# The gates' projection of a one-layer block: f32 products against three products of rounded parts

## The reference, cut to what matters

```
hx = modulate(rms_norm(x), shift, scale)       # 256 tokens x 2048
hc = modulate(rms_norm(ctx), ...)              # 256 context tokens x 2048
px = hx @ w_in                                 # 2048 x 10720
pc = hc @ w_in[:, :MIX_IN]
g_a, g_b = split(px[..., MIX_IN:], 2)          # the gates: 4096 columns, latent tokens only
yx_a = rwkv7_mixer(px[..., :RWKV_IN], ...)     # needs the final state of the context scan
yx_b = gla_mixer(px[..., RWKV_IN:MIX_IN], ...)
m = sigmoid(g_a) * (yx_a @ w_rwkv_up) + sigmoid(g_b) * (yx_b @ w_gla_up)
x = x + gx1 * rms_norm(m @ w_out)
x = x + gx2 * rms_norm(swiglu(modulate(rms_norm(x), ...)))
```

## Time and profile before

| | us |
|---|---|
| median of 3 runs | 2163.39 (2159.5 to 2163.41) |
| the profiled execution, its own time | 2161.05 |
| its span, first to last instruction | 2159.3 |
| PE busy in the span | 2020.6 (94%) |
| GLA phase, PE's first gates product to its last | 579.7 to 770.1 |
| preparation, first product to the last stored | 773.2 to some 924 |

### The profile page before, as it was taken

The page is one execution under the profiler, slowest core; times in us unless marked ns, Lnnn a source line. Parts: engine busy times, 40 slices in busy tenths (PEclk is TensorE's granted clock), DMA queues, the critical chain, the costliest instruction groups (busy, mean ns, idle before and its releaser), DMA issues. The chain is left out here.

```text
span 2159.3 us, 35926 instructions
## 1 busy us (share of the span) xinstructions
PE 2020.6 (94%) x15475; PEld 1651.2 (76%) x15475; DVE 1245.3 (58%) x1150; ACT 808.1 (37%) x895; POOL 249.9 (12%) x125
## 2 busy tenths in 40 slices
PE   5899999999999989967889899999999999999998
PEld 3367888888788866656788688778888888888886
DVE  3355666665556347768888486554445455444445
ACT  2232111212263235445554465443334333433333
POOL 0023121312304034301000020000000000000000
PEclk9899999999999999989999999999999999999999
DMA  8988889887554389967442678536555555555553
GB/s 305 382 284 313 315 316 322 290 318 270 153 143 124 88 233 312 297 151 195 93 92 57 113 228 323 178 98 192 184 187 194 186 185 192 194 202 192 193 195 115
DMA packets 355505, 453.62 MB, mean 210 GB/s; under 512 B 106062, under 2 KB 261054, under 8 KB 338094
## 3 DMA queue, kind: packets, MB, share of 16 engines
q1 hardware_dynamic: 347760, 440.59, 64.4%
q10 hardware_dynamic: 7614, 11.10, 1.4%
HBM read 413.43 MB, written 38.22 MB: 209 GB/s over the span
## 5 line engine op out<-in xcount | busy, mean ns | idle before, releaser
L220 DVE TENSOR_TENSOR f_w_lo<-t_w_raw,f_w_hi 128x2048 fp32r<-128x2048 f32 x132 | 302.4, 2292 | 361.5 <-ACT f_w_hi L214 361.5
L214 ACT ACTIVATE f_w_hi<-t_w_raw 128x2048 fp32r<-128x2048 f32 x132 | 252.9, 1916 | 436.0 <-PE pf L2926 288.0
L2924 PE MATMUL pf<-f_w_hi,h 128*128 128x512 f32 x704 | 276.3, 392 | 1.5 <-DVE h L2745 1.5
L2925 PE MATMUL pf<-f_w_lo,h 128*128 128x512 f32 x704 | 274.8, 390 | 0.0
L2926 PE MATMUL pf<-f_w_hi,h 128*128 128x512 f32 x704 | 274.7, 390 | 0.0
L214 ACT ACTIVATE p_w_hi<-h_w_raw 128x2048 fp32r<-128x2048 f32 x48 | 89.3, 1910 | 333.2 <-DVE stage L761 252.1
L906 DVE SCALAR_TENSOR_TENSOR late_acc<-h_of_x,siluc,late_acc 128x2048 f32<-128x2048 f32 x60 | 160.6, 2677 | 46.9 <-DMA h_of_x<-in_ada_w 45.2
L2975 PE MATMUL d_out<-f_w_hi,hid 128*128 128x512 f32 x704 | 176.3, 390 | 0.3 <-DVE f_w_lo L220 0.3
L264 PE MATMUL p_in<-h,p_w_hi 128*128 128x512 f32 x448 | 174.3, 389 | 0.0
L266 PE MATMUL p_in<-h,p_w_lo 128*128 128x512 f32 x448 | 174.3, 389 | 0.0
L265 PE MATMUL p_in<-h,p_w_hi 128*128 128x512 f32 x448 | 174.3, 389 | 0.0
(11 more groups left out here) (419 smaller groups left out, 3404.9 us busy)
## 6 DMA issues: line engine op xcount, KB each, us to landing
h_of_x<-in_ada_w SPq DMA_DIRECT2D x64, 1024.0 KB, 5.6
h_w_raw<-in_w_in SPq DMA_DIRECT2D x48, 1024.0 KB, 7.6
t_w_raw<-in_ffn_w_gate SPq DMA_DIRECT2D x44, 1024.0 KB, 5.2
t_w_raw<-in_ffn_w_up SPq DMA_DIRECT2D x44, 1024.0 KB, 5.2
t_w_raw<-in_ffn_w_down SPq DMA_DIRECT2D x44, 1024.0 KB, 4.9
h_w_raw<-in_ada_w SPq DMA_DIRECT2D x32, 1024.0 KB, 10.5
gate_w<-in_w_in SPq DMA_DIRECT2D x30, 1024.0 KB, 6.0
t_w_raw<-in_w_out SPq DMA_DIRECT2D x16, 1024.0 KB, 6.0
```

Of the source, the lines that this page charges most:

```text
L214: act.activation(self.hi[:, m % self.S, 0:w], self.raw[:, s, 0:w], ACT.Copy)\
L220: eng.tensor_tensor(self.lo[:, m % self.S, 0:w], self.raw[:, s, 0:w], b32(self.hi[:, m % self.S, 0:w]), ALU.subtract)\
L2924: pe.matmul(o, h2[:, 0, k, rows], fring.hi[:, s, at], start=k == 0, stop=False)
L2925: pe.matmul(o, h2[:, 0, k, rows], fring.lo[:, s, at], start=False, stop=False)
```

## The change

The gates' products become three products of rounded parts, like the rest.

- `h` is kept through the later phases as its two fp32r parts, in a new order [128, ctx or x, part, 16 k, 256 tokens]. The rejoining (L744, L779) goes. In the input projection, the 512 columns of one part of `h` are now two runs of 256 (ctx and x).
- The gates' weights come in 64 granules of 128x1024 (512 KB, rows of 1 KB): a granule holds 4 k-blocks of two tiles. Each granule is made `hi` by ACT (four of them by DVE) and `lo` in place by POOL (50 of them) or DVE (14). There are five slots for raw granules and three for `hi`: `hi` of granule n waits until granule n-3 is used.
- PE's order: in the GLA phase 96 products ahead of the levels, 16 behind each, 64 behind them, which stand between the output products; in the preparation 48 ahead, 16 in each pair, 32 behind; 16 in the scan. A product is now three instructions of 256 columns.
- In the GLA phase ACT's and DVE's work ahead of the levels is put in another order (both directions' Abs and Exp ahead of both Ln), and the norm behind the levels goes head by head.

```diff
-            hx = alloc(ph_hx, "h_of_x", [P, KT, SEQ])
+            h = alloc(ph_hx, "h", [P, 2, 2, KT, SEQ], f32r)
...
 def phase_w_in(nc, A, env):
...
-                pool.tensor_tensor(hx[:, KH:], b32(h_hi)[:, KH:, CTX:], b32(h_lo)[:, KH:, CTX:], ALU.add).then_inc(s_hx, 1)
...
-                                    last = mm3(pe, o, ring.hi[:, s, at], ring.lo[:, s, at], h_hi[:, kk, ts],
-                                               h_lo[:, kk, ts], kk == 0, kk == KT - 1)
+                                    last = mm3(pe, o.rearrange("p (a t) -> p a t", a=2), ring.hi[:, s, at],
+                                               ring.lo[:, s, at], h[:, :, 0, kk, :], h[:, :, 1, kk, :], kk == 0,
+                                               kk == KT - 1)
...
 class Gates:
...
-    STAGES = 4
-    SCAN = 1
-    AHEAD = 2
+    STAGES, RAW, SPLIT = 4, 5, 3
+    HI_VECTOR = [4, 5, 6, 7]
+    LO_VECTOR = [0] + list(range(13, 28, 2)) + [37, 39, 41, 61, 63]
...
+    def wait_raw(self, eng, n):
...
+        if n >= self.SPLIT:
+            eng.wait_ge(self.used, n - self.SPLIT + 1)
+    def hi(self, act, n):
+        self.wait_raw(act, n)
+        act.activation(self.high[:, n % self.SPLIT], self.place(n), ACT.Copy).then_inc(self.hi_scalar, 1)
+    def lo(self, eng, n):
+        eng.wait_ge(*self.hi_done(n))
+        eng.tensor_tensor(self.low_place(n), self.place(n), b32(self.high[:, n % self.SPLIT]), ALU.subtract)\
+           .then_inc(self.lo_done(n)[0], 1)
...
-            mm = pe.matmul(self.banks[t % nb][:, 0:SEQ], tiles[:, slot, k * P:(k + 1) * P], self.hx[:, k, :],
-                           start=k == 0, stop=k == KT - 1)
+            last = self.mm3(pe, self.banks[(f - self.first) % nb][:, 0:SEQ], self.high[:, n % self.SPLIT, cols],
+                            self.low_place(n)[:, cols], self.h[:, 0, k, :], self.h[:, 1, k, :], k == 0,
+                            k == KT - 1)
...
 def phase_rwkv_pre(nc, A, out, env):
...
             @block.gpsimd
...
+                gates.lo(pool, 38)
                 pool.wait_ge(s_lx, 80)
...
+                gates.lo(pool, 40)
                 neighbours(0)
                 neighbours(1)
+                gates.lo(pool, 42)
+                gates.lo(pool, 43)
                 for j in range(PAIRS):
...
+                    gates.lo(pool, 44 + 2 * j)
...
+                    gates.lo(pool, 45 + 2 * j)
                     if j + 2 < PAIRS:
                         neighbours(j + 2)
...
             @block.scalar
...
                    act.activation(nrm[:, b, :], nrm[:, b, :], ACT.Sqrt).then_inc(s_nrm, 1)
+                    gates.hi(act, 45 + 2 * j)
                     if j + 2 < PAIRS:
                         middle(j + 2)
...
+                    gates.hi(act, 46 + 2 * j)
...
             @block.tensor
             def _(pe):
-                gates.multiply(pe, 0, lead)
+                gates.multiply(pe, 8 * PRE_PARTS, 48)
...
-                    gates.multiply(pe, lead + per * j, per // 2)
+                    gates.multiply(pe, 8 * PRE_PARTS + 48 + 16 * j, 8)
...
 def phase_gla(nc, A, out, env):
...
             @block.gpsimd
...
                 for n in range(LEVELS):
+                    gates.lo(pool, 12 + 2 * n)
                     pool.wait_ge(s_e, 2 * n + 1)
                     pool.tensor_tensor(E[:, n % 2, 0], k[:], E[:, n % 2, 0], ALU.mult).then_inc(s_K, 1)
+                for n in range(28, PRE_PARTS + 1):
+                    gates.lo(pool, n)
...
             @block.scalar
...
                 for n in range(LEVELS):
+                    gates.hi(act, 12 + 2 * n)
                     for part in range(2):
...
+                    gates.hi(act, 13 + 2 * n)
...
             @block.vector
...
                     if n >= 1:
                         select(n - 1, gm[:, n - 1, :].bitcast(mybir.dt.uint32).unsqueeze(1).broadcast_to([P, GH, P]))
+                    gates.lo(dve, 13 + 2 * n)
...
             @block.tensor
...
                     level(n, E[:, n % 2, 0], E[:, n % 2, 1], n == LEVELS - 1)
-                    gates.multiply(pe, 112 + 14 * n, 14)
+                    gates.multiply(pe, 96 + 16 * n, 16)
```

More of the change, by code:

```diff
@@ L634 @@
 GLA_GATES = 18
+GATE_UNITS = [(2 * n, 2) for n in range(KT - 1)] + [(2 * KT - 2, 1), (2 * KT - 1, 1)]
+GATE_W = 1024
+GATE_PARTS = [(f, n, at) for f, n in GATE_UNITS for at in range(0, KT, GATE_W // (P * n))]
+PRE_PARTS, SCAN_PARTS = 36, 62
 def first_w_in(A):
@@ new lines, in __init__ @@
+        self.low = nc.alloc_sbuf_tensor_at("gate_w_lo", [P, self.RAW, GATE_W], f32r, offset=at)
+        self.high = nc.alloc_sbuf_tensor_at("gate_w_hi", [P, self.SPLIT, GATE_W], f32r, offset=at + 4 * self.RAW * GATE_W)
+        self.stage_at = env["late_at"] + 12 * 1024
+        self.stage = nc.alloc_sbuf_tensor_at("gate_stage", [P, self.STAGES, SEQ], f32, offset=self.stage_at)
+        new = nc.alloc_semaphore
+        self.ahead_landed = new(name="gate_ahead_landed")
+        self.landed = [new(name=f"gate_w_landed{n}") for n in range(self.RAW)]
@@ new lines, in __init__, with begin @@
+        self.hi_scalar, self.hi_vector = new(name="gate_w_hi_by_scalar"), new(name="gate_w_hi_by_vector")
+        self.lo_gpsimd, self.lo_vector = new(name="gate_w_lo_by_gpsimd"), new(name="gate_w_lo_by_vector")
+        self.used, self.made = new(name="gate_w_used"), new(name="gate_first_of_two_made")
+        self.copied = new(name="gate_copied")
+        self.stored = [new(name=f"gate_stored{n}") for n in range(self.STAGES)]
+    def begin(self, first, banks):
+        self.first, self.banks = first, banks
@@ new lines, in copy @@
+    def copy(self, act, f):
+        if f % 2 == 0 and f < 2 * KT - 2:
+            act.wait_ge(self.made, f // 2 + 1)
+        else:
+            act.wait_ge(self.used, 1 + max(n for n, part in enumerate(GATE_PARTS) if part[0] <= f))
+        if f >= self.STAGES:
+            act.wait_ge(self.stored[f % self.STAGES], 16 * (f // self.STAGES))
+        act.activation(self.stage[:, f % self.STAGES], self.banks[(f - self.first) % len(self.banks)][:, 0:SEQ], ACT.Copy)\
+           .then_inc(self.copied, 1)
@@ L1101, in _ @@
                 load(1)
-                for t in range(2):
-                    gates.load(sp, t + 2)
-                    gates.store(sp, t)
+                for n in range(41, 47):
+                    gates.load(sp, n)
+                gates.store(sp, 18)
+                gates.store(sp, 19)
                 for j in range(PAIRS):
@@ L1464, in _ @@
                         sp.dma_start(g[:], yb_d).then_inc(sm("gla_in", 0), 16)
-                        for t in range(Gates.SCAN):
-                            gates.store(sp, t)
+                        gates.store(sp, 2 * KT - 1)
                         raw.prefetch_all(sp, *first_merge(A))
@@ L1637, in ends @@
                     if (c, d) == (0, 0):
-                        gates.copy(act, 0)
+                        gates.copy(act, 2 * KT - 1)
                 def output(c, d):
@@ L2151, in _ @@
                     dve.tensor_tensor(qb[d][:], qb[d][:], q[:], ALU.mult).then_inc(s_qbm, 1)
+                decay(0)
+                running(0)
+                to_end(0)
+                decay(1)
+                keys(0)
+                running(1)
+                to_end(1)
+                keys(1)
                 def diff(n):
```

489 lines of the change are left out of this document (313 added, 176 removed).

## The result

The changed kernel takes 2226.24 us (median of 4 runs, 2223.7 to 2227.92) against 2163.26 us for the kernel before in the same comparison: a ratio of 1.0291, 95% interval 1.0271 to 1.031. It is slower by 63 us. The profiled execution took 2225.87 us, its span is 2224.1. I had forecast 2203 us, in a range of 2126 to 2232.

The account below looks back on a forecast made before the run. It took PE as the bound in GLA's levels and a chain through ACT, POOL and DVE in the preparation's pairs; terms summed to +41.5 us on 2161.05, 2202.6, forecast 2203 us with the median's 2.3 us offset noted, range 2126 to 2232.

Parts of the forecast that it names:

- PE sets the time after all: Rival for the whole kernel: PE's work is the bound, 43 us come back less 8, 2126 us; chance 0.23.
- The subtractions are hidden: Rival for the whole kernel: DVE and POOL hide the subtractions, the chains stay, +3.5, some 2165 us; chance 0.15.
- The products: Gates' products in all stages: 0.348 us each instead of 0.432, saving 43 us of PE time over 512.
- the lower bound of -4: GLA's levels: the lower bound of their term, with PE needing 7.35 us a level and no exclusion.
- `h` in two runs: Input projection: 1344 instructions reading two runs of 256 columns cost 0.006 us more each, +8 us (0 to 13).
- GLA ahead of the levels: GLA before its levels: freed PE time is spent waiting for a chain, 0 us (-15 to +5).
- A level: GLA's levels: subtractions on POOL and DVE raise 7.83 to 9.3 us in seven periods, +10 us (-4 to +15).
- the preparation's end: End of the preparation: 32 products at 0.348 us instead of 16 at 0.432, +4 us.
- Behind the levels: GLA after its levels: 64 shorter products give -5 us, POOL's nine subtractions fit in; at worst +2.
- the loads' new order: Loads of the gates' weights: queue waits move from a tile to a granule, costed at nothing.
- The start: Preparation's start: POOL's subtractions of granules 40, 42, 43 and 44 delay the first dr, +8 us (1.5 to 9).
- A pair: Preparation's pairs: POOL's subtractions delay the chain by 2.5 us a pair (0 to 4.4), seven times, +17.5 us.

Follow-up runs that it names:

- the run of two products: The changed kernel with the second of each gates product's three instructions (high part of weights by low part of h) left out: 2215.53 us, 1.0235.
- the run of none: The changed kernel with all 64 subtractions for the gates' weights left out, the third product reading the high part instead: 2171.98 us, 1.0039.
- the last run above: The kernel before, with both u put ahead of both dr in POOL's order in each pair of the preparation: 2159.02 us, 0.9978.
- the run that was to show it: The changed kernel, preparation's start reordered: ACT's gate copies and middle taps ahead of high parts 41 to 44, DVE's subtraction of 41 behind the first mixing: 2226.11 us.

## Why the prediction was right, and where its sizes were not

The direction and the mechanism were right: without the subtractions 54 of the 63 us are gone, and put into the old kernel alone they cost 38 us there. "PE sets the time after all" fell with the run of two products. "The subtractions are hidden" fell with the run of none. That the sum is no further off owes something to luck: 8 us counted for a cost that isn't there made up for part of the 31 that it lacked.

- *The products*: 0.36 us instead of 0.348, and a subtraction of POOL's takes 2.34 us undisturbed instead of 2.2. In the levels PE's work is 7.61 us (the period without differences), not 7.35, and the periods without subtractions take 7.97 against 7.83 before, so the lower bound of -4 didn't exist.
- *`h` in two runs*: +8 forecast, 0 measured. I had taken it from a stretch that mixes shapes; where the 512s stand alone its surplus isn't there.
- *GLA ahead of the levels*: 0 forecast, +11 in this profile, +5 to +11 over executions. Without subtractions it is +2.4 (573.30 to 658.85, 85.6 us against 83.2), and in none of them do PE's 15 us come back. How the rest divides between the subtractions and the high part that waits for PE stays open.
- *A level* (+10, measured +11.2), *the preparation's end* (+4, measured +3.6): as worked out, though 5.8 and 3.42 make 9.2 and not 9.3, and the differences stand in six periods and not in seven, which grew by 1.95 us each in the mean instead of 1.47.
- *Behind the levels* (-5, measured -6.3): PE's part as worked out. That POOL's nine subtractions fit into 44 us, at worst +2, was not: three of them lie over DVE's products for `y`, and that shows in the next term.
- *The gap between the stages* had no term; +8.3. Without subtractions 1.8 us of it are left (4.90 against 3.12), so some 6.5 go with the subtractions, most of it by the stretched products for `y` (10.43 instead of 4.35 us). I had also costed the loads' new order at nothing "because no chain above waits for them"; the end of a stage waits for them. The load's place alone is worth 3 us; the two overlap, since the load stands behind `y`.
- *The start*: +8 forecast, +11.5 measured, but for another reason in the main. Without subtractions 7.8 to 8.2 us remain, which by the trace lie with the high parts on ACT's queue (argued, since the run that was to show it moved another wait in); the subtractions have 3 to 4.
- *A pair*: +2.5 us forecast, +3.4 measured. Its cause is as forecast (with no subtraction the pair is at its old 14.6): 2.8 us of it are DVE's stretched steps. Its sum lacked two links. An ACT table load of 1.28 us between gate copy and sigmoids (813.83) changes no number. The square sums do, by 0.5 us: PE's wait for `ks` is followed by the lower clock, at which bonus, gate and low-rank products take 8.5 us instead of 4.7 at the upper one (the same products in the last run above, 836.30 to 841.0), and the square sums stand behind them. In the changed kernel that 0.5 us is all that the late square sums add, by PE's wait and the clock together; in the old kernel with two subtractions they add 2.6.

What the sum lacked, 23 us by the scan's start: the stage's end 8, GLA's first part 11, pairs and start 11, less 8 for the two runs that cost nothing. The steps that failed are "ahead of the levels: 0", the subtractions behind the levels taken as fitting, the loads costed at nothing and the two runs of `h` costed at 8; pairs and start were mis-sized.

## What to carry to other kernels

A product that gets cheaper on one engine by work on two others has to be priced in the stage's chain. Where DVE and POOL both work for that chain, add their two-input operations up, and count a one-input operation of POOL too when DVE's has two. Do the same where a stage ends, not only in its loop: here the subtractions behind the levels delayed the next stage. Then ask of each wait that grows whether TensorE is behind it: here its granted clock was 0.50 after such waits, and waits and clock together made the square sums late by 0.5 us a pair in one kernel and by 2.6 in another. Before moving an operation into an engine's idle time, look at what the other engine does there.

## What was not expected of the hardware

- The exclusion is not shared in turns: a POOL multiplication of 2.41 us took 7.25 while DVE ran seven two-input operations one behind the other, six of which began after it.
- A one-input operation of POOL (2.90 us) let DVE's two-input `ks` in after 1 us (870.76 plus 1.14 less 0.42 is 871.48, POOL's start 870.46); a two-input one kept DVE's difference of 0.68 us waiting until 0.55 us behind its end.
- An operation of DVE's with one tensor input was held too: `kx`, 0.48 us undisturbed, took 2.60 at 830.70 beside POOL's third subtraction at the preparation's start, and 2.59 to 2.61 in four other runs.
- In the changed kernel PE waited for `ks` once in each of seven pairs, 2.24 to 4.85 us, and each time the granted clock was 0.50 for the next products; in the kernel before, whose longest wait there was 1.31 us, it was 1.00 over all the pairs.
- Executions of the same code differ by up to 6 us in GLA's first part.
